# Hybrid decoder block: the expert gathers of a batch issued alternately, u row then v row, behind both ring waits

## The chip, the core and the metric

The kernel runs on one core of a Trainium2 chip. A core has TensorE (matrix products, called PE in the profile, with PEld for its weight loads), VectorE (DVE), ScalarE (ACT), GpSimd (POOL) and SyncE (SP). They run side by side, each through its own list of instructions, and wait for one another by semaphores. Data come from the device memory through 16 DMA engines. A gather whose row numbers are computed on the chip is issued by POOL.

The metric is the device time of one execution in microseconds (us). Lower is better.

## What is computed

One decoder layer on 256 tokens of width 2048: an attention sub-layer, and then the expert sub-layer (PEER) that the change touches. For each token and each of 8 heads, two short score vectors pick 16 of 16384 experts. An expert is one row of table u and one row of table v, 2048 float32 numbers each.

```python
def expert_block(s0):                       # 128 tokens at a time
    hs = lax.dynamic_slice_in_dim(hf, s0, PEER_TOKEN_BLOCK, 0)
    es = lax.dynamic_slice_in_dim(ef, s0, PEER_TOKEN_BLOCK, 0)   # experts, 8 heads x 16
    gs = lax.dynamic_slice_in_dim(gf, s0, PEER_TOKEN_BLOCK, 0)   # their gates
    act = jax.nn.gelu(jnp.einsum('cd,ced->ce', hs, u[es]))
    return jnp.einsum('ce,ced->cd', gs * act, v[es])
```

So a v row is needed only after the dot product of the u row of the same expert, its gelu and its gate.

## The kernel before

The attention part and the projections ahead of the experts fill the first 1220 us. The rest is the expert stage, which the change touches.

**Units, batches, gathers.** The 128 tokens of a block lie on the 128 partitions. A *unit* is one head of one block of tokens: 8 heads and 2 blocks make 16 units. A unit has 16 experts per token (TOPK), handled in 4 *batches* of 4 (BATCH). For each expert `e`, one indirect DMA gathers a u row for each of the 128 tokens (1 MB), and another one a v row. So a batch has 8 gathers, a unit 32, the stage 512.

**Rings.** The u rows land in a ring of 8 buffers (`Urow`), the v rows in another of 8 (`Vrow`), so that each holds two batches. `u_in[k]` and `v_in[k]` tell that buffer k has landed. `u_free` counts the u rows that DVE has read, `v_free` the v rows that PE has read. Both counters start at 8.

**POOL** (`unit`, lines 598 to 613) waits for the row numbers of the next unit (`idx_ready`), copies them (line 602), and then goes through the 4 batches: it waits on `u_free`, issues 4 u gathers, waits on `v_free`, issues 4 v gathers. It waits for the batch two before: u for its u rows to be read, v for its v rows.

**DVE** (`unit`, lines 1678 to 1698) takes the u rows of a batch one by one as they land (dot product with `h2`, line 1691), then does a quarter of the top-16 search for the *next* unit (`parts[b]()`), and then multiplies the gelus of the batch by the gates (`coef`, line 1686). The last quarter (`experts`, lines 1655 to 1672), behind the u rows of the fourth batch, writes the row numbers of the next unit, `idx_next` (line 1668).

**ACT** (lines 832 to 846) computes the four gelus of a batch (line 839) and, from `coef`, one diagonal 128x128 matrix for each expert (line 845).

**PE** (lines 1183 to 1190) multiplies each diagonal matrix by its v row, 4 products of 512 columns for each expert. The profile counts each as two passes, so a batch is 32 passes. They add up in PSUM over all the 8 units of a block. After the eighth unit the result is copied out (line 853) and normalised on DVE (lines 1700 to 1706) before DVE goes on to the u rows of the second block. This place is called the switch below.

Of the kernel before, what the change touches and what calls it, by code (L numbers as in the profile page):

```python
# [52 lines left out]
PH, NK, TOPK = 8, 128, 16  # L53
RING = 8
BATCH = 4
# [37 lines left out]
def build(nc, x, c, positions, ada_w, ada_b, attn_pre_g, attn_post_g, w_in, cmp_pe, cmp_w1, cmp_b1, cmp_w2,  # L93
# [13 lines left out]
    u_tab = peer_u.rearrange("l e d -> (l e) d")  # L107
    v_tab = peer_v.rearrange("l e d -> (l e) d")

    with ExitStack() as ctx:  # L110
        def sem(name):
            return ctx.enter_context(nc.semaphore(name))
# [18 lines left out]
        def at(off, *dims):  # L131
            n = int(np.prod(dims))
            v = arena[:, off:off + n]
            names = ["a", "b", "c", "d", "e"][:len(dims)]
            if len(dims) > 1:
                v = v.rearrange("p (" + " ".join(names) + ") -> p " + " ".join(names), **dict(zip(names, dims)))
            return v
# [82 lines left out]
        Urow = [at(o, D) for o in slot_off[:RING]]  # L220
        Vrow = [at(o, D) for o in slot_off[RING:2 * RING]]
# [58 lines left out]
        dve_passed, pool_passed = sem("dve_passed"), sem("pool_passed")  # L280
# [37 lines left out]
        u_in = [sem(f"u_in{i}") for i in range(RING)]  # L318
        v_in = [sem(f"v_in{i}") for i in range(RING)]
        u_free, v_free = sem("u_free"), sem("v_free")  # L320
# [129 lines left out]
        def _(pool):  # L450
# [124 lines left out]
            landed = 0  # L575
# [23 lines left out]
            def unit(u, now):  # L599
                pool.wait_ge(idx_ready, u + 1)  # L600
                pool.sem_inc(pool_passed, 1)
                pool.tensor_copy(idx_now[:, now, :], idx_next[:, :]).then_inc(idx_taken, 1)  # L602
                pool.wait_ge(idx_taken, u + 2)
                pool.sem_inc(pool_passed, 1)
                for b in range(TOPK // BATCH):
                    for tab, ring, free, landed in ((u_tab, Urow, u_free, u_in), (v_tab, Vrow, v_free, v_in)):

                        pool.wait_ge(free, u * TOPK + (b + 1) * BATCH)
                        pool.sem_inc(pool_passed, 1)
                        for e in range(b * BATCH, (b + 1) * BATCH):  # L610
                            pool.indirect_dma_start(  # L611
                                ring[e % RING], None, tab,
                                bass.IndirectOffsetOnAxis(ap=idx_now[:, now, e:e + 1], axis=0)).then_inc(landed[e % RING], 16)
            pool.wait_ge(sc_out, 8)
            pool.wait_ge(h2_ready, NT)
            with pool.Fori(0, PH) as i:
                for k in range(2):
                    unit(i * 2 + k, k)
# [1126 lines left out]
```

## Time and profile before

| | us |
|---|---|
| median of 3 runs | 2543.59 |
| lowest and highest of them | 2540.73, 2543.63 |
| span of the profiled execution | 2542.4 |
| PE busy | 2051.8 (81%) |
| DVE busy | 1338.4 (53%) |
| POOL busy | 764.2 (30%) |
| ACT busy | 438.9 (17%) |
| chain that ended last: PE, DMA, issue, DVE, POOL | 38%, 29%, 10%, 10%, 9% |

The busy shares are means over the whole span. In the second half PE and the DMA engines are both busy most of the time. The time of an instruction on POOL is that of writing a gather's orders, not that of the transfer; when the row has landed is told apart, by the time from issue to landing.

### The profile page before, as it was taken

What the parts mean: (1) busy time and instruction counts of PE and PEld (TensorE: products, weight loads), DVE (VectorE), ACT (ScalarE), POOL (GpSimd) and SP (SyncE); (2) the same over time, 40 slices, a digit from 0 to 9 for tenths busy, and PEclk for the clock granted to TensorE, in tenths of its full rate; (3) what the DMA queues carried; (4) which work ended last, traced back from release to release, by engine and by line L of the source; (5) the groups of instructions that cost most, each with busy time, mean ns of one, the idle gap of its engine ahead of it and who ended that gap; (6) DMA issues with size and microseconds to landing.
All of it is one profiled execution on the core that took longest, in us unless ns stands there. A gap on an engine that the chain in (4) does not pass through costs nothing.

```text
span 2542.4 us, 19623 instructions
## 1 busy us (share of the span) xinstructions
PE 2051.8 (81%) x5897; PEld 1095.6 (43%) x5897; DVE 1338.4 (53%) x2241; ACT 438.9 (17%) x911; POOL 764.2 (30%) x751
## 2 busy tenths in 40 slices
PE   2697999989898778969687778787758788887786
PEld 0232443436676666769333333333323333333332
DVE  5777005701445765464565555565556555655544
ACT  0000000101333323333111111111111111111110
POOL 2111001000001320000544365444544465444551
PEclk8899999997656999989788888888879888888888
DMA  9999659942000443525799999999999999999996
GB/s 347 347 358 413 219 163 378 354 132 83 33 0 1 170 169 133 199 91 198 308 416 415 423 413 417 419 416 423 414 414 392 422 418 411 419 414 423 415 416 277
DMA packets 163863, 779.89 MB, mean 307 GB/s; under 512 B 15304, under 2 KB 23660, under 8 KB 87788
## 3 DMA queue, kind: packets, MB, share of 16 engines
q0 software_dynamic: 92800, 645.96, 62.0%
q1 hardware_dynamic: 69008, 129.65, 14.7%
q10 hardware_dynamic: 2016, 3.80, 0.4%
q8 instruction: 20, 0.33, 0.1%
q14 instruction: 19, 0.16, 0.0%
HBM read 777.22 MB, written 2.13 MB: 307 GB/s over the span
## 4 chain that ended last, share of the span: by engine, by line
PE 38%; DMA 29%; issue 10%; DVE 10%; POOL 9%; SPq 2%; ACT 1%; DVEq 0%; POOLq 0%; ACTq 0%
DMA arena<-in_peer_u_dram,idx_now 22%; PE PS L911 13%; PE PS L1188 10%; POOL arena L611 8%; DMA arena<-in_ada_w_dram 3%; PE PS L896 3%; DMA arena<-in_w_in_dram 3%; PE PS L898 3%; PE PS L897 3%; DVE arena L1271 1%; SPq L394 1%; PE PS L982 1%; DVE w_lo L1540 1%; PE PS L1018 1%; PE PS L1011 1%
## 5 line engine op out<-in xcount | busy, mean ns | idle before, releaser
L1188 PE MATMUL PS<-arena 128*128 128x512 f32 x2048 | 1025.2, 665 | 282.8 <-ACT arena L845 282.8
L1691 DVE CUSTOM_DVE_ANT_0 arena<-arena 128x2048 f32<-128x2048 f32 x256 | 586.5, 2293 | 490.4 <-DMA arena<-in_peer_u_dram,idx_now 489.7
L1188 PEld LDWEIGHTS PS<-arena 128*128 128x128 f32 x2048 | 433.7, 215 | 874.4 <-issue 540.0
L911 PE MATMUL PS<-arena 128*128 128x512 f32 (+1 forms) x912 | 396.1, 595 | 22.3 <-DMA arena<-in_w_in_dram 21.7
L611 POOL DMA_INDIRECT arena<-in_peer_v_dram,idx_now x256 | 317.0, 1238 | 274.5 <-PE PS L1188 205.1
L611 POOL DMA_INDIRECT arena<-in_peer_u_dram,idx_now x256 | 317.7, 1241 | 97.8 <-issue 73.1
L911 PEld LDWEIGHTS PS<-arena 128*128 128x128 f32 x912 | 175.5, 194 | 242.2 <-issue 201.8
L1540 DVE TENSOR_TENSOR w_lo<-w_raw,w_hi 128x1024 fp32r<-128x1024 f32 x96 | 134.8, 1415 | 148.8 <-ACT w_hi L764 147.8
L839 ACT ACTIVATE act_g<-dots 128x4 f32<-128x4 f32 x64 | 13.1, 205 | 946.4 <-DVE dots L1691 946.4
L602 POOL COPY idx_now<-idx_next 128x16 uint32<-128x16 uint32 x16 | 3.7, 229 | 574.2 <-DVE idx_next L1668 574.2
L1247 DVE SCALAR_TENSOR_TENSOR arena<-arena,csil 128x2048 f32<-128x2048 f32 x60 | 141.1, 2352 | 44.5 <-DMA arena<-in_ada_w_dram 44.1
L764 ACT CAST w_hi<-w_raw 128x1024 fp32r<-128x1024 f32 x96 | 100.5, 1050 | 204.5 <-DMA w_raw<-in_peer_w_q_dram 67.9
L465 POOL DMA_DIRECT2D arena<-in_ada_w_dram x64 | 34.9, 545 | 312.1 <-DVE arena L1250 159.0
L845 ACT ACTIVATE arena<-ident,coef 128x128 f32<-128x128 f32 x256 | 81.5, 389 | 113.6 <-DVE coef L1686 113.6
L664 ACT ACTIVATE arena<-PS 128x512 f32 (+2 forms) x52 | 27.9, 588 | 360.9 <-PE PS L911 343.5
L1271 DVE SCALAR_TENSOR_TENSOR arena<-arena,csil 128x512 f32<-128x512 f32 x112 | 76.0, 746 | 13.4 <-DMA arena<-in_ada_w_dram 13.2
L1250 DVE TENSOR_SCALAR arena<-arena,csil 128x2048 f32<-128x2048 f32 x4 | 5.1, 1287 | 146.1 <-PE PS L886 145.2
L896 PE MATMUL PS<-h2T_hi,w_hi 128*128 128x256 f32 x256 | 73.3, 286 | 3.5 <-issue 3.5
L897 PE MATMUL PS<-h2T_lo,w_hi 128*128 128x256 f32 x256 | 73.2, 286 | 0.0
L898 PE MATMUL PS<-h2T_hi,w_lo 128*128 128x256 f32 x256 | 73.1, 285 | 0.0
L880 PE MATMUL PS<-ident,arena 128*128 128x128 f32 x156 | 29.8, 354 | 52.9 <-DVE arena L1608 22.0
L896 PE MATMUL PS<-w_hi,oT_hi 128*128 128x512 f32 x128 | 52.4, 409 | 23.5 <-DVE w_lo L1540 23.5
(241 smaller groups left out, 1981.0 us busy)
## 6 DMA issues: line engine op xcount, KB each, us to landing
arena<-in_ada_w_dram POOLq DMA_DIRECT2D x96, 1024.0 KB, 9.7
arena<-in_w_in_dram SPq DMA_DIRECT2D x112, 512.0 KB, 10.5
w_raw<-in_w_out_dram SPq DMA_DIRECT2D x32, 512.0 KB, 3.4
w_raw<-in_peer_w_q_dram SPq DMA_DIRECT2D x32, 512.0 KB, 3.5
w_raw<-in_w_branch_nsa_dram SPq DMA_DIRECT2D x16, 512.0 KB, 3.6
w_raw<-in_w_branch_mla_dram SPq DMA_DIRECT2D x16, 512.0 KB, 3.5
arena<-in_cmp_w_dram SPq DMA_DIRECT2D x8, 512.0 KB, 3.9
arena<-in_peer_u_dram,idx_now POOLq DMA_INDIRECT x256, 16.0
```

The costliest lines, as they stand in the source:

```text
L611: pool.indirect_dma_start(ring[e % RING], None, tab, bass.IndirectOffsetOnAxis(ap=idx_now[:, now, e:e + 1], axis=0)).then_inc(landed[e % R ...
L764: nc.scalar.copy(w_hi[:, m % SPLIT, :, :], w_raw[:, m % SPLIT, :, :]).then_inc(hi_ready, 1)
L845: nc.scalar.activation(diag[e % 8], ident[:, :], ACT.Copy, scale=coef[:, e:e + 1]).then_inc(diag_ready, 1)
L896: nc.tensor.matmul(dst, a_hi, b_hi, start=start, stop=False)
L897: nc.tensor.matmul(dst, a_hi, b_lo, start=False, stop=False)
L898: return nc.tensor.matmul(dst, a_lo, b_hi, start=False, stop=stop)
L911: ins = nc.tensor.matmul(PS[:, (n % 2) * 2 + t, 0:cols], lhs[:, kk, t * P:(t + 1) * P], wring[:, (m + w) % WSLOTS, k, 0:cols], start=(kk = ...
L1188: ins = nc.tensor.matmul(PS[:, bank + k, :], diag[e % 8], Vrow[e % RING][:, k * NC:(k + 1) * NC], start=False, stop=False, skip_group_chec ...
L1247: ins = v.scalar_tensor_tensor(out=acc, in0=w, scalar=csil[:, j:j + 1], in1=acc, op0=ALU.mult, op1=ALU.add)
L1271: ins = v.scalar_tensor_tensor(out=acc, in0=w, scalar=csil[:, j:j + 1], in1=acc, op0=ALU.mult, op1=ALU.add)
L1540: v.tensor_tensor(w_lo[:, m % SPLIT, :, :], w_raw[:, m % SPLIT, :, :], w_hi[:, m % SPLIT, :, :].bitcast(F32), ALU.subtract).then_inc(lo_re ...
L1691: v.tensor_tensor_reduce(row, row, h2[:, t, :], 1.0, 0.0, ALU.mult, ALU.add, dots[:, e:e + 1]).then_inc(u_free, 1)
```

## The change

POOL waits for both counters ahead of a batch and then issues the 8 gathers in the order u, v, u, v, ... The waits' values, the gathers and their number are the same.

```diff
                 for b in range(TOPK // BATCH):
-                    for tab, ring, free, landed in ((u_tab, Urow, u_free, u_in), (v_tab, Vrow, v_free, v_in)):
-
-                        pool.wait_ge(free, u * TOPK + (b + 1) * BATCH)
-                        pool.sem_inc(pool_passed, 1)
-                        for e in range(b * BATCH, (b + 1) * BATCH):
+                    pool.wait_ge(u_free, u * TOPK + (b + 1) * BATCH)
+                    pool.sem_inc(pool_passed, 1)
+                    pool.wait_ge(v_free, u * TOPK + (b + 1) * BATCH)
+                    pool.sem_inc(pool_passed, 1)
+                    for e in range(b * BATCH, (b + 1) * BATCH):
+                        for tab, ring, landed in ((u_tab, Urow, u_in), (v_tab, Vrow, v_in)):
                             pool.indirect_dma_start(
                                 ring[e % RING], None, tab,
                                 bass.IndirectOffsetOnAxis(ap=idx_now[:, now, e:e + 1], axis=0)).then_inc(landed[e % RING], 16)
```

The order on POOL at the start of a unit, before (`idx_now` holds the row numbers; `in_peer_u_dram` and `in_peer_v_dram` are the tables u and v):

```order
L602 COPY idx_now<-idx_next 128x16 [waits idx_ready]
L603 REGISTER_ALU
L608 ISA [waits idx_taken]
L611 DMA arena<-in_peer_u_dram,idx_now 128x2048 [waits u_free]
L611 DMA arena<-in_peer_u_dram,idx_now 128x2048 x3
L611 DMA arena<-in_peer_v_dram,idx_now 128x2048 [waits v_free]
L611 DMA arena<-in_peer_v_dram,idx_now 128x2048 x3
L608 REGISTER_ALU
L611 DMA arena<-in_peer_u_dram,idx_now 128x2048 [waits u_free]
```

And in the changed kernel, the same place (the second half of the batch is left out):

```order
L602 COPY idx_now<-idx_next 128x16 [waits idx_ready]
L603 REGISTER_ALU
L606 ISA [waits idx_taken]
L612 DMA arena<-in_peer_u_dram,idx_now 128x2048 [waits u_free,v_free]
L612 DMA arena<-in_peer_v_dram,idx_now 128x2048
L612 DMA arena<-in_peer_u_dram,idx_now 128x2048
L612 DMA arena<-in_peer_v_dram,idx_now 128x2048
...
L606 REGISTER_ALU
L612 DMA arena<-in_peer_u_dram,idx_now 128x2048 [waits u_free,v_free]
```

What moved: the wait on `v_free` stands ahead of the first u gather, and the fourth u gather is the seventh of its batch, where it was the fourth. No instruction of another engine moved.

## Rows read from the trace of the kernel before

**Rows 1.** Stretches: busy us and instructions, granted clock, DMA share, GB/s.
```profile
core 0: us, PE busy (x) PEld busy (x) DVE busy (x) ACT busy (x) POOL busy (x), PEclk, DMA share, GB/s
...
1302.00:1382.00 80.00, 65.15 (x128) 27.43 (x128) 46.02 (x72) 11.64 (x27) 41.78 (x33) 0.88 1.01 417
...
1863.00:1943.00 80.00, 55.96 (x118) 24.51 (x119) 46.26 (x68) 14.91 (x29) 39.71 (x33) 0.81 0.97 394
```

**Rows 2.** Waits of POOL in the expert stage: total us, times, longest us.
```profile
POOL idx_now L602 <- DVE idx_next L1668: 265.4, 15, 18.4
POOL arena L611 <- PE PS L1188: 206.0, 33, 12.4
```

**Rows 3.** Timeline, a second batch: start us, us, what, [idle before, releaser].
```profile
1410.35 2.29 DVE L1691 CUSTOM_DVE_ANT_0 arena<-arena 128x2048 f32<-128x2048 f32 x1 [7.81 <-DMA arena<-in_peer_u_dram,idx_now]
...
1411.29 2.17 POOL L611 DMA_INDIRECT arena<-in_peer_u_dram,idx_now  x1 [0.30 <-issue]
...
1417.81 2.29 DVE L1691 CUSTOM_DVE_ANT_0 arena<-arena 128x2048 f32<-128x2048 f32 x1 [0.18 <-DMA arena<-in_peer_u_dram,idx_now]
...
1422.89 15.70 PE L1188 MATMUL PS<-arena 128*128 128x512 f32 x32 [4.17 <-ACT arena L845]
...
1439.40 1.39 POOL L611 DMA_INDIRECT arena<-in_peer_v_dram,idx_now  x1 [9.80 <-PE PS L1188]
```

**Rows 4.** Page, costliest groups: the products with the v rows.
```profile
L1188 PE MATMUL PS<-arena 128*128 128x512 f32 x2048 | 1025.2, 665 | 282.8 <-ACT arena L845 282.8
```

**Rows 5.** Timeline, end of one unit and start of the next.
```profile
1457.57 2.29 DVE L1691 CUSTOM_DVE_ANT_0 arena<-arena 128x2048 f32<-128x2048 f32 x1 [0.19 <-DMA arena<-in_peer_u_dram,idx_now]
...
1462.89 0.23 POOL L602 COPY idx_now<-idx_next 128x16 uint32<-128x16 uint32 x1 [18.37 <-DVE idx_next L1668]
...
1464.09 0.96 POOL L611 DMA_INDIRECT arena<-in_peer_u_dram,idx_now  x1 [0.97 <-POOL idx_now L602]
```

**Rows 6.** Single gathers: duration ns, start us, and time to landing.
```profile
L611 POOL DMA_INDIRECT arena<-in_peer_u_dram,idx_now x1: 1053/1053/1053, 1221.9 to 1221.9; - x1
...
DMA to landing us min/median/max: 5.5/5.5/5.5
...
L611 POOL DMA_INDIRECT arena<-in_peer_v_dram,idx_now x1: 2311/2311/2311, 1232.1 to 1232.1; - x1
...
DMA to landing us min/median/max: 14.2/14.2/14.2
...
L611 POOL DMA_INDIRECT arena<-in_peer_u_dram,idx_now x1: 937/937/937, 1932.2 to 1932.2; - x1
...
DMA to landing us min/median/max: 14.0/14.0/14.0
...
L611 POOL DMA_INDIRECT arena<-in_peer_v_dram,idx_now x1: 938/938/938, 2495.7 to 2495.7; - x1
...
DMA to landing us min/median/max: 23.9/23.9/23.9
```

**Rows 7.** Timeline around the switch between the blocks of tokens.
```profile
1864.47 0.23 POOL L602 COPY idx_now<-idx_next 128x16 uint32<-128x16 uint32 x1 [17.73 <-DVE idx_next L1668]
...
1882.27 1.86 ACT L853 COPY arena<-PS 128x2048 f32<-128x2048 f32 x1 [16.02 <-PE PS L1188]
...
1891.95 2.29 DVE L1691 CUSTOM_DVE_ANT_0 arena<-arena 128x2048 f32<-128x2048 f32 x1 [0.19 <-DVE gate_now L1679]
...
1921.03 2.19 POOL L611 DMA_INDIRECT arena<-in_peer_v_dram,idx_now  x1 [12.45 <-PE PS L1188]
...
1951.53 0.23 POOL L602 COPY idx_now<-idx_next 128x16 uint32<-128x16 uint32 x1 [12.11 <-DVE idx_next L1668]
```

**Rows 8.** Timeline, end of the kernel, and the span.
```profile
core 0 of [0], span 2542.4 us
...
2509.68 2.29 DVE L1691 CUSTOM_DVE_ANT_0 arena<-arena 128x2048 f32<-128x2048 f32 x1 [0.20 <-DMA arena<-in_peer_u_dram,idx_now]
...
2512.97 15.60 PE L1188 MATMUL PS<-arena 128*128 128x512 f32 x32 [2.88 <-ACT arena L845]
```

## The prediction

> **What bounds the kernel now.** I read the stretches first. In a stretch of one unit in the expert stage (80 us) the DMA engines show a share of 1.01 at 417 GB/s [rows 1], in fifteen of the sixteen units: they never pause. PE is busy 65 us of the 80, DVE 46, POOL 42, so none of these is full. A gather moves 1.05 MB, so at 417 GB/s it takes 2.51 us, a batch of 8 takes 20.1 us and a unit of 32 takes 80.4 us. The copies of the row numbers agree: from 1462.89 [rows 5] to 1864.47 [rows 7] five units pass in 401.6 us, 80.3 each. The stage is bound by the transfers. All of POOL's waits (265 us for row numbers and 206 us for PE [rows 2]) are covered, since enough gathers are queued. What matters is how much is still queued when each wait ends, because that is what the change takes from.
>
> **What the change does to the queue.** (1) Before, the fourth u row of a batch lands four gathers (10 us) ahead of its last v row. Now it lands one gather (2.5 us) ahead. All that hangs on it (dots, gelu, coefficients, PE, the row numbers of the next unit) starts 7.5 us later against the queue. (2) Before, POOL issued the u rows of batch B+2 as soon as DVE had read batch B, and only the v rows waited for PE. Now all eight wait for PE. The number of gathers is the same, and two counters waited for in a row cost POOL some 0.3 us a batch at most, beside waits of many us: nothing.
>
> **Prices, from rows.** Call L the time at which the last gather of a batch lands.
>
> Route to PE. The fourth u row lands at L - 2.5, and its dot starts 0.2 us behind the landing. In the row of a second batch, that dot starts at 1417.81 and PE at 1422.89, 5.1 us later (gelu, a quarter of the search, coefficients, diagonal matrix) [rows 3]. PE needs 1025.2 / 64 = 16.0 us a batch [rows 4]; the batch shown took 15.7. POOL's v gather started 0.8 us behind PE's end (1438.59 to 1439.40) [rows 3]. So POOL can issue batch B+2 at L - 2.5 + 0.2 + 5.1 + 16.0 + 0.8 = L + 19.6. But at that time DVE is at the last dot of batch B+1, which started at L + 17.8. A gather issued inside a dot takes longer: 2.17 us, where others take 0.94 (issued at 1411.29, done 0.8 us behind the end of the dot) [rows 3]. The dot ends at L + 20.1, the issue at L + 20.9, and without it the issue would have ended at L + 20.5. I add 0.4: L + 20.0.
>
> Route to the row numbers. From the last dot's start at 1457.57 the copy comes 5.3 us later, and the first gather of the new unit 6.5 us later (1464.09) [rows 5]. So the first gather of a unit starts at L - 2.5 + 0.2 + 6.5 = L + 4.2, where L is that of the last batch.
>
> Restart. No unit of before starts from an empty queue, but the stage's first does: its first gather started at 1221.9 and the eighth landed at 1232.1 + 14.2 = 1246.3, 24.4 us later [rows 6]. Behind the switch the queue had nearly run out: issued from 1921.03 [rows 7], the eighth landed at 1932.2 + 14.0 = 1946.2, 25.1 us later, of which some 1.2 are a first issue lengthened by a dot (2.19 us): 23.9. I take 24.0. The lower bound is 23.1: the first row landed 5.5 us behind its issue [rows 6], and seven more follow at 2.51. The upper bound is 25.1.
>
> The Trainium skill (DMA: Bandwidth & Descriptors, section Anatomy of one DMA) fits a GpSimd transfer as about 2.0 us plus bytes over 436 GB/s. That would be an estimate of 2.0 + 8 x 2.4 = 21.2 us for a restart, where the rows here show 5.5 for one gather and 24.4 for eight: the rows decide, and by the page's figure the sum below would end near 2650. The skill (SBUF — State Buffer) also has VectorE and GpSimd share a port pair that one locks against the other for a whole instruction; the 2.17 us issue beside a dot agrees, and the 0.4 above is all that it makes here.
>
> **The sum over one unit.** L of the last batch of the unit before is 0. First batch: 4.2 + 24.0 = 28.2. Second: POOL may issue it from about 20 to 21, well ahead of 28.2 - 1.4, so it follows at 28.2 + 20.1 = 48.3. Third: it needs the v buffers of the first, so 28.2 + 20.0 + 24.0 = 72.2, while the transfers alone would allow 68.4. Fourth: issued from 48.3 + 19.6 = 67.9 it would allow 91.9, and the transfers 72.2 + 20.1 = 92.3: 92.3. The next unit's first batch needs the row numbers at 96.5; the third's v buffers come free near 93. So a unit takes 92.3 where it took 80.4: **+11.9 us**, 8.1 from the row numbers and 3.8 from the ring.
>
> - 15 units: 15 x 11.9 = 178.5.
> - First unit: its row numbers come as before, only the ring's 3.8.
> - Switch: DVE is free for the second block's u rows 9.7 us behind the end of PE (1882.27 to 1891.95) [rows 7]. Now PE ends at about +20, so DVE starts at 29.7, takes four landed rows in 8.9 and is done at 38.6. A usual unit is done with them at 28.2 - 2.5 + 0.2 + 2.3 = 28.2, 10.4 earlier; less the 0.4 for the blocked issue, the third batch is late by 10.0. Before, this unit took 1951.53 - 1864.47 = 87.1, so 6.7 over the others [rows 7]. Net +3.3.
> - End: the last v row landed at 2495.7 + 23.9 = 2519.6 [rows 6], the last dot started at 2509.68 and the span ended 32.7 us behind that [rows 8]. Now the last u row lands 2.5 ahead of the last v row instead of 9.9: +7.4. PE starts 3.3 us behind the last dot's start, when all v rows are there.
>
> Together 178.5 + 3.8 + 3.3 + 7.4 = 193.0. On the profiled 2542.4 that is 2735.4. The median of the runs lies 1.2 above the profiled span, so **2737 us**, 7.6% longer. With 23.1 for a restart a unit takes 27.3 + 43.1 + 20.1 = 90.5 and the sum is 15 x 10.1 + 2.9 + 3.3 + 7.4 = 165, so 2709. With 25.1 it takes 94.5, and the sum is 15 x 14.1 + 4.9 + 3.3 + 7.4 = 227, so 2771. The forecast's own range is 2705 to 2775.
>
> **Rivals.**
> 1. *Only the row numbers cost, the ring is covered.* If PE took 12 us a batch instead of 16, or the restart from a queue that has only just run out were free (the third batch's gap is only some 2 us long), the third batch would follow at 20.1. A unit is then 28.2 + 60.3 = 88.5, +8.1, and the sum 121.5 + 0 + 3.3 + 7.4 = 132, so 2676; with a cheap restart at the row numbers too, 2650. For it: the page's smaller fixed price. Against it: the restart at 1921.03 came from just such a short gap and cost as much as the long one, and PE's batches show no 12. Chance 0.18.
> 2. *More than that.* PE's gap grows in two of four batches. If its batches then take 17 us (the stretch's granted clock fell from 0.88 to 0.81 around the switch's idle time [rows 1]), and issues are blocked by dots as at 1921.03, a unit takes 29.3 + 46.1 + 20.1 = 95.5, and the sum is 15 x 15.1 + 5.9 + 3.3 + 7.4 = 243, so 2787. Chance 0.09.
> 3. *Not slower.* The queue still covers all, and alternating tables lets the engines move more: the change then costs the end's 7.4 and gains 512 gathers times what each saves. It is level from 0.015 us a gather (2.51 to 2.495); at 2.42 us (an assumed 434 GB/s) it gains 46, so 2505. For it: the bytes in flight are the same, and the sum above needs each route to be late by only a few us. Against it: the cover has to hold 28.2 us in 20.1, and the rows of a stretch show 417 at a full share. Chance 0.03: 0.02 faster, 0.01 within.
>
> That the change doesn't do what it says is excluded by the order on POOL: both waits stand ahead of the first u gather, and u and v alternate.
>
> **How the numbers follow.** Forecast 0.70, rivals 0.18, 0.09, 0.03. A measurement of this kernel tells about 0.2% (5 us) from no change. Slower by more: 0.97. For the range I leave out half of the second rival and some of the lower part of the first: 2665 to 2775.
>
> **What would show it.** Each unit at 92 us by the copies of the row numbers; DMA share about 0.87 in the stage, with two gaps a unit, one at the row numbers (some 5 to 8 us) and one ahead of the third batch (some 2 to 4); POOL's gathers waiting for PE ahead of the third and fourth batch only; DVE's u rows 5 us apart; the last PE batch starting behind the last v row. I am wrong if the third batch follows the second with no pause (rival 1), if PE's batches grow to 17 us (rival 2), or if the share stays at 1.0 (rival 3).

## The result, and the profile after

The changed kernel takes 2737.03 us (median of 4 runs, 2731.16 to 2739.12), the kernel before in the same comparison 2543.61 us (median of 4, 2540.73 to 2544.23). The ratio is 1.0758, with a 95% interval of 1.0740 to 1.0775: 7.6% slower. The profiled execution has a span of 2737.5 us.

The page of the changed kernel: the GB/s in 40 slices of the span, and the costliest groups of the expert stage (busy us, mean ns of one | idle us before, and what ended it). Lines behind 605 carry numbers one higher than before.

```profile
span 2737.5 us, 19623 instructions
...
GB/s 351 354 377 399 155 245 398 209 93 46 0 1 152 170 138 169 120 167 392 346 368 344 390 349 361 367 379 356 356 351 342 374 340 396 348 375 346 397 348 227
...
L1189 PE MATMUL PS<-arena 128*128 128x512 f32 x2048 | 1017.8, 660 | 482.1 <-ACT arena L846 459.8
L1692 DVE CUSTOM_DVE_ANT_0 arena<-arena 128x2048 f32<-128x2048 f32 x256 | 586.4, 2292 | 684.0 <-DMA arena<-in_peer_u_dram,idx_now 683.8
```

PE's work on the v rows is the same (1017.8 us, 1025.2 before [rows 4]), but its idle time ahead of them grew from 282.8 to 482.1 us. That is 199 us, about all that the kernel lost. DVE's dots also take what they took and wait longer. The engines do the same work; it is the transfers that pause.

Stretches, columns as in [rows 1]: first the whole expert stage, then one ordinary unit, then the pieces of that unit around its two pauses.

```profile
1220.00:2737.50 1517.50, 1021.50 (x2057) 431.70 (x2055) 747.53 (x1155) 190.72 (x434) 668.10 (x528) 0.83 0.87 355
...
1313.00:1405.00 92.00, 62.20 (x129) 26.41 (x128) 45.85 (x74) 11.76 (x27) 39.70 (x33) 0.85 0.89 365
1312.00:1314.00 2.00, 1.97 (x5) 0.57 (x3) 1.93 (x7) 0.20 (x1) 0.00 (x0) 1.00 0.15 61
1314.00:1319.00 5.00, 1.66 (x4) 0.87 (x5) 2.76 (x8) 2.10 (x5) 1.23 (x3) 1.00 0.00 0
1319.00:1321.00 2.00, 2.00 (x6) 0.88 (x5) 0.00 (x0) 1.97 (x3) 1.69 (x2) 1.00 0.84 246
...
1361.00:1364.00 3.00, 0.18 (x1) 0.00 (x0) 2.07 (x11) 0.44 (x2) 1.71 (x2) 0.96 0.21 44
...
1367.00:1380.00 13.00, 12.66 (x30) 5.37 (x28) 6.06 (x5) 0.00 (x0) 5.11 (x4) 0.99 1.01 408
```

The DMA share is 0.87 over the stage and 0.89 over the unit, where a unit had 1.01 before [rows 1]. At 1314 to 1319 it is 0.00: the row numbers of the next unit are not there until 1316.39. At 1361 to 1364 it is 0.21: the third batch waits for PE. Between the pauses the engines are as full as before (1.01).

The waits of POOL in the stage: total us, times, longest.

```profile
POOL idx_now L602 <- DVE idx_next L1669: 517.7, 16, 312.1
POOL arena L612 <- PE PS L1189: 419.1, 46, 19.3
...
POOL arena L612 <- DVE dots L1692: 19.8, 1, 19.8
```

The first line holds one wait of 312.1 us from ahead of the stage; the other 15 make 205.6 us, fewer than the 265.4 before [rows 2]. POOL waits less for the row numbers and yet the kernel is slower: what a wait costs is told by what is still queued when it ends, not by its length. The second line's 46 waits are three for each unit and one for the first, so the second batch waits for PE too. That wait costs nothing: it ends at 1332.15, while the first batch is landing until 1341.7.

The chain at the start of a unit and at its third batch, from the timeline (start us, us, what, [idle before, releaser]):

```profile
1311.08 2.29 DVE L1692 CUSTOM_DVE_ANT_0 arena<-arena 128x2048 f32<-128x2048 f32 x1 [2.68 <-DMA arena<-in_peer_u_dram,idx_now]
...
1316.39 0.23 POOL L602 COPY idx_now<-idx_next 128x16 uint32<-128x16 uint32 x1 [15.09 <-DVE idx_next L1669]
...
1317.70 0.96 POOL L612 DMA_INDIRECT arena<-in_peer_u_dram,idx_now  x1 [1.08 <-issue]
...
1344.33 16.84 PE L1189 MATMUL PS<-arena 128*128 128x512 f32 x32 [12.99 <-ACT arena L846]
...
1361.99 0.94 POOL L612 DMA_INDIRECT arena<-in_peer_u_dram,idx_now  x1 [17.16 <-PE PS L1189]
...
1380.47 1.18 POOL L612 DMA_INDIRECT arena<-in_peer_u_dram,idx_now  x1 [7.45 <-PE PS L1189]
```

And the last gather of the batch ahead of this unit and of its four batches, each with the time from its issue to its landing:

```profile
L612 POOL DMA_INDIRECT arena<-in_peer_v_dram,idx_now x1: 937/937/937, 1300.4 to 1300.4; - x1
DMA to landing us min/median/max: 13.1/13.1/13.1
...
L612 POOL DMA_INDIRECT arena<-in_peer_v_dram,idx_now x1: 940/940/940, 1327.9 to 1327.9; - x1
DMA to landing us min/median/max: 13.8/13.8/13.8
...
L612 POOL DMA_INDIRECT arena<-in_peer_v_dram,idx_now x1: 938/938/938, 1343.9 to 1343.9; - x1
DMA to landing us min/median/max: 17.7/17.7/17.7
...
L612 POOL DMA_INDIRECT arena<-in_peer_v_dram,idx_now x1: 938/938/938, 1372.1 to 1372.1; - x1
DMA to landing us min/median/max: 13.9/13.9/13.9
...
L612 POOL DMA_INDIRECT arena<-in_peer_v_dram,idx_now x1: 937/937/937, 1392.7 to 1392.7; - x1
DMA to landing us min/median/max: 13.1/13.1/13.1
```

Issue and landing added, the batches end at 1313.5, 1341.7, 1361.6, 1386.0 and 1405.8. From the end of the unit before these are 28.2, 48.1, 72.5 and 92.3 us.

The same reading of the kernel before, for the unit whose first gather starts at 1464.09 [rows 5]: the last gather of the unit ahead of it, and the eighth of its first batch.

```profile
L611 POOL DMA_INDIRECT arena<-in_peer_v_dram,idx_now x1: 937/937/937, 1443.6 to 1443.6; - x1
DMA to landing us min/median/max: 23.9/23.9/23.9
...
L611 POOL DMA_INDIRECT arena<-in_peer_v_dram,idx_now x1: 2187/2187/2187, 1476.5 to 1476.5; - x1
DMA to landing us min/median/max: 11.5/11.5/11.5
```

The queue ends at 1467.5 and the eighth lands at 1488.0, 20.5 us later and 23.9 us behind the first issue. So the kernel before issued the first gather of a unit 3.4 us ahead of the queue's end. Read in this way, its first batches take 20.8 us on average (14 ordinary units) and all its other batches 19.9. The transfers did not quite run without a pause: some 0.9 us a unit was lost already, and there was no cover left at the row numbers for the change to take.

### The profile page after: what moved, and what is told of

It reads as the page before. It is cut to its first block, busy times and chain, and to the rows that moved or that the text cites. A ratio compares the mean times of both kernels' runs of the same rounds, so it can differ in the third digit from the quotient of the medians.

```text
span 2737.5 us, 19623 instructions
## 1 busy us (share of the span) xinstructions
PE 2053.8 (75%) x5897; PEld 1101.0 (40%) x5897; DVE 1337.2 (49%) x2241; ACT 438.9 (16%) x911; POOL 793.1 (29%) x751
## 3 DMA queue, kind: packets, MB, share of 16 engines
q1 hardware_dynamic: 69008, 129.65, 13.6%
## 4 chain that ended last, share of the span: by engine, by line
PE 45%; DMA 22%; issue 11%; DVE 10%; POOL 9%; ACT 2%; SPq 1%; DVEq 0%; POOLq 0%; ACTq 0%
PE PS L1189 19%; DMA arena<-in_peer_u_dram,idx_now 16%; PE PS L912 12%; POOL arena L612 9%; PE PS L897 2%; DMA arena<-in_w_in_dram 2%; DMA arena<-in_ada_w_dram 2%; PE PS L899 2%; PE PS L898 2%; DVE arena L1272 1%; PE PS L983 1%; DVE w_lo L1541 1%; PE PS L1019 1%; SPq L394 1%; PE PS L1012 1%
## 5 line engine op out<-in xcount | busy, mean ns | idle before, releaser
L1189 PE MATMUL PS<-arena 128*128 128x512 f32 x2048 | 1017.8, 660 | 482.1 <-ACT arena L846 459.8
L612 POOL DMA_INDIRECT arena<-in_peer_u_dram,idx_now x256 | 301.8, 1179 | 514.9 <-PE PS L1189 419.1
L912 PE MATMUL PS<-arena 128*128 128x512 f32 (+1 forms) x912 | 393.3, 592 | 23.8 <-DMA arena<-in_w_in_dram 23.3
L612 POOL DMA_INDIRECT arena<-in_peer_v_dram,idx_now x256 | 362.6, 1416 | 81.4 <-issue 81.4
L940 PE MATMUL PS<-arena 128*128 128x512 f32 x128 | 65.7, 678 | 5.8 <-issue 5.8
```

The source lines that it names most:

```text
L612: pool.indirect_dma_start(ring[e % RING], None, tab, bass.IndirectOffsetOnAxis(ap=idx_now[:, now, e:e + 1], axis=0)).then_inc(landed[e % R ...
L912: ins = nc.tensor.matmul(PS[:, (n % 2) * 2 + t, 0:cols], lhs[:, kk, t * P:(t + 1) * P], wring[:, (m + w) % WSLOTS, k, 0:cols], start=(kk = ...
L1189: ins = nc.tensor.matmul(PS[:, bank + k, :], diag[e % 8], Vrow[e % RING][:, k * NC:(k + 1) * NC], start=False, stop=False, skip_group_chec ...
```

## The experiments

Theory: the stage is bound by transfers, and the change takes the cover from two routes that were hidden: fourth u row to row numbers to the next unit's first gather, and v rows to PE to the batch after next. Rivals: the joined wait costs by itself; the two losses are independent and add; PE has no part in it; u rows have to be ahead of all v rows, whatever the distance. The kernel before ran beside them: median 2534.17 us for u rows first, the two with a part of the batches alternating, and half of the products; 2536.43 us for the other four. The forecasts in full us were made on 2543.6, so below the distance from the kernel before is compared. All edits but the last are shown against the changed kernel. The lines inside POOL's loop that pick table, ring and semaphore for a gather are not shown.

### Joined waits, u rows first

```diff
-                    for e in range(b * BATCH, (b + 1) * BATCH):
-                        for tab, ring, landed in ((u_tab, Urow, u_in), (v_tab, Vrow, v_in)):
+                    for kind, k in [(s, k) for s in "uv" for k in range(BATCH)]:
```

> The changed kernel with both waits ahead of a batch, but the gathers again four u rows and then four v rows. Theory (what counts is how many gathers stand behind the fourth u row of a batch): it lands four gathers ahead of the batch's end, POOL may issue the batch after next 12.2 us behind that end, 36.2 us with a restart of 24.0, and the transfers take 40.2: nothing is lost, 2543 to 2548 us. Rival (the joined wait itself costs, since the u gathers now wait for PE): the 3.8 us a unit of the ring remain, 2604 us.

Measured: 2546.68 us, ratio 1.0044 (1.0029 to 1.0058), 12.5 us over the kernel before. The rival's 60 us are refuted, but the loss is more than the theory's 0 to 5. In the trace the ordinary units take 80.1 us ahead of the switch and 80.3 behind it, not more than the 80.5 of the kernel before; the unit at the switch takes 94.4 (1960.70 - 1866.29), where it took 87.1 [rows 7]:

```profile
1866.29 0.23 POOL L602 COPY idx_now<-idx_next 128x16 uint32<-128x16 uint32 x1 [13.01 <-DVE idx_next L1670]
...
1921.82 0.94 POOL L613 DMA_INDIRECT arena<-in_peer_u_dram,idx_now  x1 [19.42 <-PE PS L1190]
1960.70 0.23 POOL L602 COPY idx_now<-idx_next 128x16 uint32<-128x16 uint32 x1 [13.39 <-DVE idx_next L1670]
```

The u rows of the third batch wait 19.4 us for PE. Before, u rows could be issued at 1901.7 there, when DVE had read its own. So the joined wait costs where PE is late for another reason. The switch shows 7.3 us of the 12.5, the low end of the interval (7 to 15 us); where the rest lies is not shown.

### The same, with the normalisation moved

DVE's `finish(0)` goes behind the four dots of the second block's first batch.

```diff
-            def unit(u, t, last=False):
+            def unit(u, t, last=False, between=None):
...
+                    if between and b == 0:
+                        between()
                     if parts:
                         parts[b]()
...
-            finish(0)
-            with dve.Fori(0, PH - 1) as u:
+            unit(PH, 1, between=lambda: finish(0))
+            with dve.Fori(0, PH - 2) as u:
                 ch.enter(u, TOPK_STEPS + 1)
-                unit(u + PH, 1)
-                ch.leave(PH - 1)
+                unit(u + (PH + 1), 1)
+                ch.leave(PH - 2)
```

> Both waits joined and four u rows first (as in e1_u_first), with the same move of the normalisation. Theory (the 12 us that the joined wait costs there come from the switch, where the third batch waited 19.4 us for PE and the unit took 94.4 us against 87.1): PE frees the v rows 8.9 us earlier, and the time falls by 7 to 9 us against e1_u_first, to within 5 us of the kernel before. Rival (the joined wait costs a little in every unit): no gain over e1_u_first, 12 us over the kernel before.

Measured: 2536.59 us, ratio 1.0008 (0.9993 to 1.0022), in another comparison than the 1.0044 above, but each against the kernel before. The loss of the joined wait is gone. The nearest comparison is the last experiment, the kernel before with the same move, run beside this one: 2536.71 us. In the trace the unit at the switch falls from 94.4 to 86.0 us, and the wait from 19.4 to 12.9:

```profile
1855.16 0.23 POOL L602 COPY idx_now<-idx_next 128x16 uint32<-128x16 uint32 x1 [13.42 <-DVE idx_next L1670]
...
1902.11 0.93 POOL L613 DMA_INDIRECT arena<-in_peer_u_dram,idx_now  x1 [12.88 <-PE PS L1190]
1941.13 0.23 POOL L602 COPY idx_now<-idx_next 128x16 uint32<-128x16 uint32 x1 [13.39 <-DVE idx_next L1670]
```

### Alternating in the fourth batch alone

```diff
+                    for kind, k in ([(s, k) for k in range(BATCH) for s in "uv"] if b == 3 else
+                                    [(s, k) for s in "uv" for k in range(BATCH)]):
```

> Both waits joined, u and v alternate in the fourth batch of a unit alone. Theory: the row numbers of the next unit are late (8.1 us a unit), the ring is covered: 15 x 8.1 + 3.3 at the switch + 7.4 at the end = 132, 2676 us. Rival (the row numbers are covered, only the ring's loop costs): below 2560 us.

Measured: 2670.16 us, ratio 1.0526 (1.0507 to 1.0545), 136 us over the kernel before (132 forecast; the rival, 16 at most, is refuted). In the trace the ordinary units take 87.8 us on average (88.5 forecast) and the one at the switch 101.1. One batch in four makes 136 us where all four make 193, since it alone stands ahead of the row numbers.

### Alternating in the first three batches alone

```diff
+                    for kind, k in ([(s, k) for k in range(BATCH) for s in "uv"] if b < 3 else
+                                    [(s, k) for s in "uv" for k in range(BATCH)]):
```

> Both waits joined, u and v alternate in the first three batches of a unit, the fourth has its u rows first. Theory: the row numbers come in time, but the ring's loop now runs through the first and third batch of every unit: 43.8 us from first to third, 45.0 from the third (whose share of the search is 1.4 us longer) to the next unit's first, 88.8 us a unit where the transfers take 80.4; 15 x 8.4 + 3.8 + 3 = 133, 2676 us. Rival (the two terms of the sum simply add, so that 3.8 to 4.2 us a unit remain): 2611 us.

Measured: 2673.01 us, ratio 1.0549 (1.0525 to 1.0573), 139 us over the kernel before (133 forecast). The additive rival (67 us over) is refuted: alone each half costs about 137 us, both together 193. In the trace of this kernel the row numbers come early and PE holds the first gather of every unit behind the first: at the second copy below the wait for them is 4.7 us, and POOL then waits 3.9 us more for PE. Between the two copies shown below a unit takes 87.2 us; over the six units behind the switch it is 88.8 us, the 88.8 forecast.

```profile
2205.97 0.23 POOL L602 COPY idx_now<-idx_next 128x16 uint32<-128x16 uint32 x1 [7.18 <-DVE idx_next L1671]
2293.21 0.23 POOL L602 COPY idx_now<-idx_next 128x16 uint32<-128x16 uint32 x1 [4.71 <-DVE idx_next L1671]
2297.34 0.96 POOL L614 DMA_INDIRECT arena<-in_peer_u_dram,idx_now  x1 [3.89 <-PE PS L1191]
```

### The changed kernel with half of the products

```diff
-                    for k in range(4):
+                    for k in range(2):
                         ins = nc.tensor.matmul(PS[:, bank + k, :], diag[e % 8], Vrow[e % RING][:, k * NC:(k + 1) * NC],
```

> The changed kernel with two of the four 512-column products for each v row left out (half of each v row is not used), so that PE takes 8 us a batch. Theory: the ring's loop falls to 36 us and is covered, the row numbers stay late: 28.2 + 60.3 = 88.5 us a unit, and the switch and the end get 5 and 0.4 us shorter than before: 2660 us. Rival (PE has no part in the loss): 2725 us or more, the shorter end and switch alone.

Measured: 2645.32 us, ratio 1.0442 (1.0424 to 1.0459), 111 us over the kernel before (116 forecast, 181 or more by the rival), so some 82 us less than the full change. PE's batches take 9 us, not the 8 forecast. The granted clock was 0.773 over this execution and 0.841 over the changed kernel's:

```profile
1420.91 9.23 PE L1189 MATMUL PS<-arena 128*128 128x512 f32 x16 [17.75 <-ACT arena L846]
1440.78 9.54 PE L1189 MATMUL PS<-arena 128*128 128x512 f32 x16 [10.63 <-ACT arena L846]
```

A unit takes 87.6 us on average ahead of the switch and 87.3 behind it (88.5 forecast). In all 14 ordinary units the third batch now lands 19.9 to 20.0 us behind the second: its pause is gone. PE's time is a part of the loss, though PE is busy for only 62 us of a unit's 92: it stands in the loop from v row to v buffer. The rest, the row numbers, stays.

### Three, and two, gathers behind the fourth u row

```diff
+                    for kind, k in (("u", 0), ("u", 1), ("u", 2), ("v", 0), ("u", 3), ("v", 1), ("v", 2), ("v", 3)):
```

and

```diff
+                    for kind, k in (("u", 0), ("u", 1), ("v", 0), ("u", 2), ("v", 1), ("u", 3), ("v", 2), ("v", 3)):
```

> Both waits joined, order of a batch u u u v u v v v: the fourth u row has three gathers behind it. Theory: the row numbers' first gather starts at 6.7 - 7.5 = 0.8 us ahead of the queue's end, 23.2 us to the batch's end where the transfers take 20.1, so 3.1 us a unit; the ring's loop is 38.8 us and covered; with 1 at the switch and 2.5 at the end 50 us over the kernel before. Rival (all u rows must come before all v rows, the number behind does not matter): as much as the changed kernel, +190 us.

> Both waits joined, order of a batch u u v u v u v v: the fourth u row has two gathers behind it. Theory: row numbers 25.7 us to the first batch's end (5.6 late), ring's loop from first to third batch 41.3 (1.2 late, mostly hidden behind the other), 87.1 us a unit, 6.7 over 80.4; 15 x 6.7 + 1 + 2 + 5 = 109 us over the kernel before. Rival as for three behind: +190 us.

Measured with three: 2581.8 us, ratio 1.0175 (1.0153 to 1.0196), 45 us over the kernel before (50 forecast). With two: 2669.88 us, ratio 1.0518 (1.0495 to 1.0541), 133 us over it (109 forecast). With the ends known (four behind: about 0, one behind: 193), each gather fewer costs more time, as the distance has it, though not in equal steps; the rival that only u before v matters is refuted.

With three behind, a unit takes 82.6 us (83.5 forecast): the first gather starts 0.8 us ahead of the queue's end, as forecast. With two, the forecast was 24 us short: a unit takes 87.8 us ahead of the switch and 88.7 behind it, where 87.1 was forecast, and the one at the switch takes 100.8. In the timeline of that kernel a dot starts just ahead of the fourth batch's first gather:

```profile
1541.77 2.29 DVE L1693 CUSTOM_DVE_ANT_0 arena<-arena 128x2048 f32<-128x2048 f32 x1 [2.68 <-DMA arena<-in_peer_u_dram,idx_now]
1542.02 2.85 POOL L613 DMA_INDIRECT arena<-in_peer_u_dram,idx_now  x1 [5.35 <-PE PS L1190]
...
1545.18 0.94 POOL L613 DMA_INDIRECT arena<-in_peer_u_dram,idx_now  x1 [0.30 <-issue]
```

The issue takes 2.85 us in place of 0.94, with 4.6 us left in the queue, and the batch ended 22.4 us behind the one before it instead of 19.9. I had not added this wherever a first gather could meet a dot. The units are 1.1 us longer than forecast on average, 17 us in 15 of them, and the switch has most of the rest. The trace bears the cause out: the fourth batch lands 19.8 or 19.9 us behind the third in the six units where its first issue took 0.93 or 0.94 us, and 21.1 to 22.7 us behind it in the ten where that issue took 1.7 to 2.85 us, 23 us more in all. The ten also had less queued (3.6 to 4.6 us, the six 4.9 or more); by the 24.0 us from issue to eighth landing that makes some 1 us of the 23, an estimate. The other three batches of a unit together are no longer than forecast. No run was made without the lengthened issues.

### The kernel before, with the normalisation moved

The edit is that of the second experiment, made to the kernel before.

> The kernel before, with DVE's normalisation of the first block of tokens put behind the four dots of the next unit's first batch, in place of ahead of them. PE can start that batch 8.9 us earlier. The transfers' pause of 3.5 us at the switch goes: 0.14% faster than the kernel before, ratio 0.9986. Rival (the pause is hidden elsewhere or made by the store of the first block): ratio 1.000.

Measured: 2536.71 us, ratio 0.9997 (0.9981 to 1.0013). In its trace the unit at the switch takes 83.6 us (1947.15 - 1863.51) in place of 87.1, as forecast, but the interval holds both 0.9986 and 1.000. The pause at the switch is shorter, as the trace shows; as a gain in time it is inconclusive; no version here beats the kernel before by more than can be measured.

```profile
1863.51 0.23 POOL L602 COPY idx_now<-idx_next 128x16 uint32<-128x16 uint32 x1 [18.37 <-DVE idx_next L1668]
1909.16 0.94 POOL L611 DMA_INDIRECT arena<-in_peer_v_dram,idx_now  x1 [7.56 <-PE PS L1188]
1947.15 0.23 POOL L602 COPY idx_now<-idx_next 128x16 uint32<-128x16 uint32 x1 [18.37 <-DVE idx_next L1668]
```

## Why the prediction was right

Step by step against the trace of the changed kernel:

- *What binds.* The stage was held by its transfers, and the pauses now appear in the time. Shown: share 1.01 to 0.89, PE's work unchanged. "They never pause" was slightly too strong: the first batch of a unit took 20.8 us and the others 19.9, as read above. The share for the stage was forecast as about 0.87 and is 0.87.
- *Row numbers.* The first gather of a unit was forecast 4.2 us behind the last landing. It came at 1317.70, with the landing at 1313.5: 4.2.
- *Restart.* Forecast 24.0 us from first issue to eighth landing: 1317.70 to 1341.7 is 24.0, and 1361.99 to 1386.0 is 24.0, the latter behind a pause of only some 3 us. Over the 14 ordinary units behind the first it is 23.2 to 24.3 us at the row numbers and 24.0 to 25.0 at the third batch. This was the widest unknown of the sum. The row at the switch of the kernel before decided it, as a short pause there had cost as much as an empty queue.
- *Ring.* The third batch's first gather was forecast 19.6 us behind the first batch's end, with 0.4 for a dot beside it. It came at 20.3. Two errors nearly cancelled: PE's batch behind a 13 us gap took 16.84 us and not 16.0, and the dot had ended at 1361.4, so that nothing lengthened the issue. The 16.84 is the clock: in the gap ahead of this batch, when PE had been idle for 5 us, it fell to 0.50, the lower of its two levels (1.2 GHz), and it was still there in the first half dozen us of the batch. The batch before, all at 1.00 (2.4 GHz), took 14.0:

```profile
1317.34:1331.34 14.00, 14.00 (x32) 6.00 (x32) 4.52 (x4) 3.79 (x6) 8.98 (x8) 1.00 0.85 323
1345.00:1350.00 5.00, 5.00 (x7) 2.02 (x6) 2.33 (x3) 0.16 (x1) 0.00 (x0) 0.50 1.01 419
```

- *Unit.* Ends forecast at 28.2, 48.3, 72.2 and 92.3; measured 28.2, 48.1, 72.5 and 92.3. Seven units from 1316.39 to the copy at 1962.52 give 92.3 each, the six behind the switch 91.9. That it fits to a tenth is in part luck: a batch without a pause takes 19.9 us and not 20.1, since 20.1 is the mean with the kernel's own small pauses in it, and the third batch came 24.4 us behind the second and not 23.9. The order of the two tables itself costs nothing: batches without a pause land in 19.9 us before and after.
- *Switch.* The unit took 101.95 us (1962.52 to 2064.47), 9.6 over the others; 10.0 forecast. The joined wait's part in it (94.4 against 87.1 with u rows first) lay inside that sum, and not in the ordinary units.
- *The whole.* From the first copy of row numbers to the last, the kernel grew by 178.3 us (forecast 181), from there to the end by 13.6 (forecast 12). The stage began 3.2 us later, in a part that the change does not touch (over all traces here it begins between 1214 and 1230 us). That is 195.1 in the profiled executions, against 193.0 forecast, and 191.9 without the late start.
- *A sign that was wrong.* POOL was to wait for PE ahead of the third and fourth batch only. It waits ahead of the second too (3.3 us at 1332.15), at no cost.

The rivals: *only the row numbers cost* is refuted by the pause at 1361 and by the alternation in the first three batches, which costs 139 us with the row numbers in time. *More than that* was right for one of PE's batches (16.84), but over all of them PE took 15.9 us a batch (16.0 before), so its premise of 17 failed. The lengthened first issue did show, but as a loss only with two gathers behind. *Not slower* fell with the share.

One reading of the sum needs care. I split a unit's 11.9 us into 8.1 for the row numbers and 3.8 for the ring. The experiments show that these are not two independent costs: taking the row numbers away (first three batches) saves not 8.1 us a unit but 3.5 (92.3 to 88.8), because the ring's loop through the first and third batch is nearly as long (88.8 us). The forecast for that kernel came from following each loop, and not from the split.

## What to carry to other kernels

When a stage is bound by its transfers, ask of every wait of the issuing engine how many transfers stand behind the one that it hangs on: that is its cover, and the order of the queue sets it. Follow each loop (landing, compute, buffer free, issue, landing) through its own batches and take the longest, since two loops that are late don't add. A row that others wait for belongs ahead of rows that only need it later, even where both are of the same batch.

## What the runs showed of the hardware

- From the issue of the first of 8 gathers of 1 MB to the landing of the eighth it takes some 24 us unless enough is queued ahead of it; in a full queue 8 land in 19.9. Averages over the first batches of 14 ordinary units: 23.9 us with the queue's end 4.2 us before the issue (changed kernel), 23.8 with 0.8 us still queued (three behind), 24.2 with 3.4 us still queued (kernel before). So it is not a price of the empty queue: by these rows an issue some 4 us ahead of the queue's end costs nothing (24.0 - 19.9, an estimate), and each us later costs one.
- An indirect DMA whose issue POOL begins while a dot runs on DVE ends 0.8 us behind the end of the dot and takes up to 3.0 us, not 0.94: so in all 127 lengthened issues beside a dot in the changed kernel's trace (0.80 to 0.82 us) and all 119 of the kernel before. The 102 issues there that began ahead of a dot and ran into it took 0.94 or less. With 9 us or more still queued this cost nothing (the second batches of the kernel before land in 19.9 us), with 3.6 to 4.6 us queued it cost 1.3 to 2.8 us (two behind). The Trainium skill (SBUF — State Buffer, section Who interferes with whom) has a DVE instruction with two SBUF inputs and a GpSimd instruction that reads SBUF lock a shared port pair against each other for a whole instruction; the issues that end at a fixed 0.8 us behind the end of the dot agree. That the dot would wait in its turn, where the issue came first, does not show: all 256 dots take 2.29 to 2.36 us.
